# Second FFN of a Hymba-style decoder layer: units of seven block products from unit 3, third pair of token sums one unit sooner

## The reference

```
x = x + 1/2 * SwiGLU_1(RMSNorm(x))
x = x + W_out @ concat(gla(h), dilated_attention(h)),  h = RMSNorm(x) @ W_in
x = x + 1/2 * SwiGLU_2(RMSNorm(x))
out = RMSNorm_final(x)

swiglu(x, w1, w3, w2) = (silu(x @ w1) * (x @ w3)) @ w2      # w1, w3: 1024 x 2816, w2: 2816 x 1024
```

## Time and profile before

| | us |
|---|---|
| median of 3 runs (922.87 to 923.59) | 922.9 |
| the profiled execution | 924.18 |
| its span | 922.4 |
| PE busy | 913.3 (99%) |
| DVE busy | 658.1 (71%) |
| ACT busy | 500.8 (54%) |
| POOL busy | 153.2 (17%) |

### The profile page before, as it was taken

The page is one execution under the profiler, slowest core; times in us unless marked ns, Lnnn a source line. Parts: engine busy times, 40 slices in busy tenths (PEclk is TensorE's granted clock), DMA queues, the critical chain, the costliest instruction groups (busy, mean ns, idle before and its releaser), DMA issues.

```text
span 922.4 us, 13487 instructions
## 1 busy us (share of the span) xinstructions
PE 913.3 (99%) x5132; PEld 768.6 (83%) x5132; DVE 658.1 (71%) x973; ACT 500.8 (54%) x749; POOL 153.2 (17%) x140
## 2 busy tenths in 40 slices
PE   9999999999999999999999999999999999999997
PEld 8888888888888887888778778888888888888885
DVE  6779974459988668654576747769995347999726
ACT  7757651147776336531346965747773126677423
POOL 0213239222230000000021100012310012222000
PEclk9999999999999999999999999999999999999998
DMA  7448833548884252233212022438864356887572
GB/s 297 125 105 212 191 116 117 157 122 191 211 201 114 86 178 102 92 107 106 87 47 85 8 92 91 126 80 213 196 149 139 119 143 155 196 218 169 173 130 91
DMA packets 71609, 127.69 MB, mean 138 GB/s; under 512 B 25728, under 2 KB 49024, under 8 KB 67840
## 3 DMA queue, kind: packets, MB, share of 16 engines
q1 hardware_dynamic: 30656, 101.07, 32.0%
q0 software_dynamic: 19472, 22.94, 16.3%
q10 hardware_dynamic: 21424, 2.91, 2.0%
HBM read 117.59 MB, written 2.10 MB: 130 GB/s over the span
## 4 chain that ended last, share of the span: by engine, by line
PE 89%; DVE 4%; DMA 4%; issue 1%; ACT 1%; POOL 0%; SPq 0%; DVEq 0%; ACTq 0%
PE banks L1785 18%; PE banks L1787 17%; PE banks L1786 17%; PE banks L1838 17%; PE banks L1840 9%; DMA x<-in_up 2%; DMA block_sums<-in_up 2%; PE banks L1853 1%; PE banks L1849 1%; PE banks L1851 1%; PE banks L2140 1%; PE banks L2173 1%; PE banks L2156 1%; DVE w_lo L1161 1%; DVE w_lo L1153 1%
## 5 line engine op out<-in xcount | busy, mean ns | idle before, releaser
L672 ACT ACTIVATE w_hi<-raw 128x2048 fp32r<-128x2048 f32 (+2 forms) x52 | 87.4, 1680 | 146.2 <-PE banks L1787 136.5
L1838 PE MATMUL banks<-h_both,w_hi 128*128 128x512 f32 x420 | 153.2, 398 | 0.8 <-DVE w_lo L1153 0.8
L1838 PE MATMUL banks<-tok_sums,w_hi 128*128 128x512 f32 x420 | 151.1, 392 | 0.0
L1128 DVE TENSOR_TENSOR w_lo<-raw,w_hi 128x2048 fp32r<-128x2048 f32 (+2 forms) x52 | 105.4, 2027 | 51.2 <-ACT w_hi L672 50.7
L1840 PE MATMUL banks<-tok_sums,w_lo 128*128 128x256 f32 x420 | 118.0, 281 | 0.0
L1840 PE MATMUL banks<-h_both,w_lo 128*128 128x256 f32 x420 | 117.8, 281 | 0.0
L1785 PE MATMUL banks<-g_hi,w_hi 128*128 128x512 f32 x272 | 106.1, 390 | 0.2
L1787 PE MATMUL banks<-g_hi,w_lo 128*128 128x512 f32 x272 | 105.8, 389 | 0.0
L1786 PE MATMUL banks<-g_lo,w_hi 128*128 128x512 f32 x272 | 105.8, 389 | 0.0
L1785 PE MATMUL banks<-h_both,w_hi 128*128 128x512 f32 x264 | 104.3, 395 | 0.1
L1786 PE MATMUL banks<-h_both,w_hi 128*128 128x512 f32 x264 | 102.9, 390 | 0.0
(11 more groups left out here) (277 smaller groups left out, 1931.3 us busy)
## 6 DMA issues: line engine op xcount, KB each, us to landing
raw<-in_up SPq DMA_DIRECT2D x35, 768.0 KB, 5.9
block_sums<-in_up SPq DMA_DIRECT2D x36, 256.0 KB, 3.4
block_sums<-in_up POOLq DMA_DIRECT2D x36, 256.0 KB, 5.2
x<-in_up SPq DMA_DIRECT2D x34, 256.0 KB, 3.6
x<-in_up POOLq DMA_DIRECT2D x34, 256.0 KB, 5.2
raw<-in_up SPq DMA_DIRECT2D x8, 1024.0 KB, 4.8
raw<-in_w_proj SPq DMA_DIRECT2D x8, 1024.0 KB, 4.7
raw<-in_down1a SPq DMA_DIRECT2D x8, 768.0 KB, 4.2
```

What stands on the lines that cost most here:

```text
L672: nc.scalar.activation(w_hi[slot_of(u)][:, 0:size], raw[u % 2][:, 0:size], ACT.Copy).then_inc(w_round, 1)
L1128: nc.vector.tensor_tensor(w_lo[slot_of(u)][:, 0:size], raw[u % 2][:, 0:size], w_hi[slot_of(u)][:, 0:size].bitcast(F32), ALU.subtract).then ...
L1838: nc.tensor.matmul(by_half(out), hi[:, cols], both, start=start and p == 0, stop=False, skip_group_check=True)
```

## The change

```diff
-SEVEN = {(0, 0): (5, 6, 7, 8, 9, 10, 11), (0, 12): tuple(range(10)), (2, 0): tuple(range(4, 12)),
+SEVEN = {(0, 0): (5, 6, 7, 8, 9, 10, 11), (0, 12): tuple(range(10)), (2, 0): tuple(range(3, 12)),
          (2, 12): tuple(range(10))}
-TOKEN_SUMS = {0: {1: (1,), 2: (2, 3)}, 2: {0: (1,), 1: (2, 3)}}
+TOKEN_SUMS = {0: {1: (1,), 2: (2, 3)}, 2: {0: (1, 2), 1: (3,)}}
```

## The result

| | us |
|---|---|
| before, median (4 runs) | 923.1 |
| changed, median (4 runs, 934.5 to 936.2) | 935.7 |
| ratio, 95% interval | 1.0129 [1.0117, 1.0141] |
| the profiled execution, span | 935.9, 932.9 |

The forecast was 929.5, with a range to 931.8; the median lies 3.9 us beyond that range. The sign, the places and the order of the waits are as forecast; one term of the sum, the second wait, was put at less than half of what it is. The interval of the ratio is clear of 1. The ratio is that of the record; it is not the quotient of the two medians, which would be 1.0137.

What follows compares the result with a forecast made beforehand. TensorE, busy 913.3 of 922.4 us, was taken as the bound. −1.06 for the unit, +1.65 and +4.5 for two waits and +1.5 for the clock gave +6.6, so 929.5 us from the median, range 927.7 to 931.8.

Steps and rivals of the forecast that it cites:

- the second wait: TensorE before unit 4 of the second FFN's up phase waits for the low part of its weights: 4.5 us.
- What a unit brings: Unit 3 in the second FFN's up phase, converted from eight products to seven, saves TensorE 1.06 us.
- The first wait: TensorE before unit 3 waits 1.65 us for the fourth pair of token sums, made behind unit 3's halves on VectorE.
- The chain to unit 4: Unit 4's load waits for the fourth pair; SyncE's load, GpSimd's adds and VectorE's work follow, ready at 623.0.
- GpSimd's adding leg: From GpSimd's issue of unit 4's adding DMAs to VectorE's add: 6.6 us, between ends of 5.9 and 7.75.
- The clock: TensorE's clock falls to half 2.1 us into the wait before unit 4, costing 1.5 us on work.
- full clock (1): Both waits before units 3 and 4, but TensorE's clock stays full: +5.1 us, 928.0; chance 0.22.
- Only the first wait (2): The DMA legs take 6.5 us together, so TensorE waits only before unit 3: +0.6 us, 923.5; chance 0.07.
- no wait (3): Token sums and the DMA chain come in time for units 3 and 4: −1.06 us, 921.8; chance 0.04.
- the change does nothing (4): Unit 3 stays one of eight products: 922.9 us; chance 0.01.
- the delay grows from unit to unit (5): Blocks come too late for units 5 and 6 as well, +1 to +2 us each: 931.5 or more; chance 0.08.

Runs made afterwards that it cites:

- both: Changed kernel with free_buffer's separate memory and early_sums' VectorE and ScalarE order together: 922.8 us, ratio 0.9996 against the kernel before.
- early_sums: Changed kernel with VectorE and ScalarE reordered so the fourth pair of token sums comes ahead of unit 3's low parts: 929.5 us, ratio 1.0052.
- free_buffer: Changed kernel with unit 4's block sums in memory of their own, so SyncE need not wait for the token sums: 924.7 us, ratio 1.0015.
- hold_loads: Changed kernel with SyncE holding back unit 5's blocks and raw weights until GpSimd's adding DMAs for unit 4 have landed: 931.3 us, ratio 1.0074.
- warm: Changed kernel with 72 filling matmuls on TensorE before it waits for unit 4's weights: 932.3 us, ratio 1.0091.
- hold_warm: Changed kernel with unit 5's loads held back as in hold_loads and 33 filling matmuls in the wait before unit 4: 929.6 us, ratio 1.0064.
- seven_only: Changed kernel with the old TOKEN_SUMS, unit 3 still of seven: 935.0 us, ratio 1.0121.
- hold_raw: Changed kernel with only unit 5's raw weights held back until the adding DMAs for unit 4 have landed: 932.9 us, ratio 1.0107.

## Why the prediction was half right

- *What a unit brings* (1.06): in the changed kernel unit 5 and all later units are 9.84 us apart as before, and unit 3 took 10.1 us (607.23 to 617.3), not 10.88. As a gain in the total it was not clearly seen, even in both.
- *The first wait* (1.65): 1.59 in the changed kernel, 0 with the new order in early_sums, 2.29 with the old sums. The cause, the halves of unit 3 ahead of pair 3 on VectorE, is shown by early_sums.
- *The chain to unit 4*: shown by free_buffer, which takes the one wait out of SyncE's queue and with it the whole second wait. Of its legs, SyncE to GpSimd was 5.06 us (4.45 forecast), VectorE's adds to unit 4's start 3.33 (3.3).
- *The step that failed is GpSimd's adding leg*: "I take 6.6, nearer the calm one since most of the traffic is over when the second lands". It was 11.1 in the changed kernel, and 9.7 and 10.1 in the two variants with the same loads behind it. I had seen that unit 5's loads fall "right on top of the adding DMAs", and then took a value from rows in which other loads had been issued 3.4 us or more before, or 4.0 and 4.7 us behind. hold_loads shows it: with the loads held the leg is 6.0, the second wait 4.25, the total +7.9, within the range forecast. This term alone is 4.5 of the missing 6.0; the leg from SyncE to GpSimd is another 0.6. The reason given, that most of the traffic would be over, is what failed: unit 5's raw weights, issued at 613.43, took 8.6 us to land, until some 622.
- *The clock* (1.5): it fell as forecast, and the cost was 1.8 in the trace of the changed kernel. But the reckoning was wrong, and the near figure is luck. I let a spell of 5.4 us, read from the start of the trace, begin with the fall, so that a longer wait would hide it. By that the spell would have ended at 625.5, before the work began, and cost nothing. It lasted from 620.1 to 630.4, ending 3.7 us behind the start of work. In hold_loads, with a wait of the length forecast, it ended 5.5 us behind and unit 4 was 2.6 us longer, in early_sums 5.6 and 2.6. In these traces the cost has to be counted from the restart. So hold_loads' total is in the range with a clock term 1.1 over mine.
- *Rivals*: full clock (1) is out by the rows of the clock; warm shows what it is worth. Only the first wait (2), and no wait (3), were ruled out as transfers stood; both became true when their cause was built in (free_buffer, both). That the change does nothing (4) is out: unit 3 runs at L1838. That the delay grows from unit to unit (5) was not seen in the changed kernel; small waits before later units stand in hold_warm (0.38) and both (0.5).
- *Still open*: by what rule two loads issued behind the adding DMAs hold these back by 5 us while either alone costs 1.1 or 2.3. The trace shows that GpSimd's queue stood still until 616 and slowed again from 618 to 620 while SyncE's moved; it doesn't show why. How much GpSimd's own adding DMAs for unit 5, issued at 619.63, add to the leg was not tested.

## What to carry to other kernels

When a stage starts sooner, look at every shared buffer that its loads go to. Here the load for the second unit of seven goes into scratch memory and waits there for the last token sums, and all loads behind it in the queue wait with it: that cost ten times the gain. And when a chain is shortened, don't take a transfer's time from rows in which it ran alone; look at what the new order issues within a microsecond of it. With TensorE 99% busy, a conversion worth 1 us has to be free everywhere else.

## What the runs showed of the hardware that I had not expected

The same pair of 256 KB adding DMAs from GpSimd took, from issue to use, 5.9 and 6.0 us without loads behind them (hold_warm, hold_loads), 7.6 with 1.25 MB issued 2.4 us behind (early_sums), and 9.7 to 11.1 with the same 1.25 MB issued 0.3 to 0.4 us behind (seven_only, warm, changed). In the changed kernel GpSimd's queue had 3 packets from 612 to 616, and SyncE's 290.

TensorE's clock at half came in every run whose wait before unit 4 was 3.9 us or longer and unfilled. The waits of 1.6 us, and one of 2.29 in seven_only, left it at 1.00. Back at work, the half clock lasted 3.4 (hold_raw) to 5.6 us (early_sums) more, and unit 4 took 1.7 to 2.6 us longer than 9.84. Waits of 5.68 and 9.15 us were followed by the shorter spells, one of 3.92 by the longest: in these six traces a longer wait did not mean a longer spell.
